# Even mixer of a two-block network: causal mask by TensorE, modulation rows by ScalarE, another order of sums, taps and output pieces

## The chip, the cores and the metric

The program runs on one core of a Trainium2 chip. Its engines are TensorE (PE in the profile, with its weight loads as PEld), VectorE (DVE), ScalarE (ACT), GpSimd (POOL) and SyncE (SP), which here issues nearly all DMAs. The metric is the device time of one execution in microseconds (us), lower is better.

## The reference, cut to what matters

The program computes two transformer-like blocks on 256 tokens of width 1024. The change lies in one stage of the first block, the even mixer, and in the modulation products that are computed beside it:

```python
mod = cond @ mod_w[layer] + mod_b[layer]            # six vectors of 1024 for each layer
h = rms_norm(x, mix_norm_g[layer]) * (1 + sc1) + sh1

def even_mixer(h, ...):
    a_val, a_gate, q, k, v = split(h @ in_w)         # 512 columns each
    u = a_val * sigmoid(a_gate)
    u = causal_dwconv(u, dw_w, dw_b)                 # 31 taps
    u = silu(layer_norm(u, ln_g, ln_b))
    q, k = rms_norm(heads(q)), rms_norm(heads(k))    # 8 heads of 64
    o = stick_breaking_attention(q, k, v)
    return concatenate([u, o]) @ out_w

# stick_breaking_attention, for one block of 128 queries
z = q @ k.T * scale
causal = kpos < qpos
log_1m = where(causal, log_sigmoid(-z), 0)
between = reverse_cumsum(log_1m) - log_1m
wts = where(causal, exp(log_sigmoid(z) + between), 0)
```

After the mixer come a gated mixture of experts (MoE), a second layer with another mixer, and the second block. They are not touched.

## The kernel before, in words

Every engine runs a list of its own, written out by hand, in order; semaphores join them. There is no scheduler. An instruction that waits holds up all that stands behind it on its engine.

Weights come from a plan (`weight_plan`): pieces of 1 MB, in the order in which TensorE uses them, through eight buffers. SyncE issues the DMA of piece i as soon as TensorE has finished with piece i - 8 (L593). A piece that is "split" is rounded by ScalarE (`act_round`, L633, two halves) and its rest computed by VectorE (`dve_half`, L650, two halves) before TensorE uses it three times over; pieces of `mod_w` are used raw.

Modulation is cut into 24 halves, numbered q. For each: TensorE multiplies the two weight pieces into four 32-row strips (`mod_half`, 8 matmuls), someone copies the 512-wide bank into a row buffer with two places (`mod_copy`, L668 on VectorE, L770 on ScalarE), TensorE sums the strips (`mod_sums`, one matmul of 512 columns for a gate, four of one column otherwise), and VectorE makes the final vector (`mod_vector`, L678 for a gate, else L682 to L688). Halves 4 to 15 run beside the even mixer. Before, VectorE copies rows 4 to 11 and ScalarE rows 12 to 15. A copy of row q waits until the sum of q - 2 is done; the products of q + 1 wait for the vector of q - 1 (`mod_half`).

In the even mixer the scores of all heads stand in six banks, z 0 to 2 for even heads and z 3 to 5 for odd ones; one of each three (2 and 5) holds the second half of the keys against the second half of the queries. ScalarE computes |z|, exp and log (L860 to L868), VectorE adds max(z, 0) to make L and multiplies the diagonal blocks by a 0/1 mask (`below`), TensorE adds the running sums onto the banks ("R", matmuls with `ntri` and `nones`), VectorE adds -1e30 above the diagonal (`negdiag`), ScalarE takes exp (L873, L874), TensorE multiplies by the values (semaphore `even_o`), ScalarE and VectorE split the result (catTh L877, catTl).

All this time VectorE works through the convolution: 31 taps, each four operations on 128x256 (L1246 with x4 per tap). The calls `conv(n)` place n taps in VectorE's list. When all are done TensorE computes mean and variance over channels, VectorE and ScalarE normalise (reciprocal L1446), and TensorE multiplies by the output weights: two pieces for rows 512 and up (from the attention), two for rows 0 to 511 (from the convolution).

Of the kernel before, what the change touches and what calls it, by code (L numbers as in the profile page):

```python
# [13 lines left out]
T = 256  # L14
# [70 lines left out]
UPTO = {"start": 2, "norm": 4, "z": 8, "R": 10, "o": 12, "x1": 14, "m0": 16, "odd": 24}  # L85


def weight_plan():
# [14 lines left out]
    def mod(l, v):  # L103
        for half in range(2):
            by_cols("mod_w", (l,), D, v * D + half * 512, 512, False)

# [106 lines left out]
    "even_dve": {"even_u": 2, "even_ss0": 1, "even_qn0": 1, "even_ss1": 1, "even_qn1": 1, "even_L": 6, "even_d": 6,  # L213
# [39 lines left out]
def mod_bank(q):  # L253

    if q < 4:
        return 4 + q
    if q == 18:
        return 1
    return (6 if q < 10 else 2 if q < 14 else 4 if q < 16 else 2) + q % 2
# [57 lines left out]
def program(nc, A, out):  # L317
    ctx = ExitStack()
    with ctx:
# [434 lines left out]
        def act_program(e):  # L754
# [66 lines left out]
            def even():  # L821
# [47 lines left out]
                for n, i in enumerate((2, 0, 1, 5, 3, 4)):  # L869
                    d = diag(L[:, i, :], i % 3)  # L870
                    e.wait_ge(*V("even_d", n + 1))
                    if i % 3 < 2:
                        e.activation(off(L[:, i, :]), off(banks[i][:, :]), ACT.Exp)  # L873
                    e.activation(d, d, ACT.Exp).then_inc(S("even_w"), 1)  # L874
# [11 lines left out]
                e.activation(sq[:, 0:T], banks[1][:, 0:T], ACT.Sqrt, scale=1.0 / 512, bias=eps).then_inc(S("even_usd"), 1)  # L886
                e.wait_ge(*V("even_un", 1))
# [5 lines left out]
                mod_copy(e, 12, copy)  # L893
# [330 lines left out]
        def dve_program(e):  # L1224
# [119 lines left out]
            def even():  # L1344
# [60 lines left out]
                for q in range(4, UPTO["z"]):  # L1405
                    mod_copy(e, q, e.tensor_copy)
                    conv(1)
                    if q > 4:
                        mod_vector(e, own, q - 1)
                for par in range(2):  # L1410
                    e.wait_ge(*V("even_ln", par + 1))
                    for i in range(3 * par, 3 * par + 3):
                        seen = own.did(stt(L[:, i, :], banks[i][:, :], 0.0, L[:, i, :], ALU.max, ALU.add))
                        own.see(seen)
                        d = diag(L[:, i, :], i % 3)
                        tt(d, d, bc(C["below"], d.shape[1]), ALU.mult).then_inc(S("even_L"), 1)
                mod_vector(e, own, 7)
                conv(2)
                for n, i in enumerate((2, 0, 1, 5, 3, 4)):
                    d = diag(L[:, i, :], i % 3)  # L1420
                    e.wait_ge(*V("even_R", 3 * (n // 3) + 3))
                    tt(d, diag(banks[i][:, :], i % 3), bc(C["negdiag"], d.shape[1]), ALU.add).then_inc(S("even_d"), 1)
                mod_copy(e, 8, e.tensor_copy)
                conv(1)
                mod_copy(e, 9, e.tensor_copy)
                conv(1)
                for i in range(2):
# [3 lines left out]
                       ).then_inc(S("even_ol"), 1)  # L1431
                mod_vector(e, own, 8)
                mod_vector(e, own, 9)
                conv(2)
                mod_copy(e, 10, e.tensor_copy)
                split_only(out(512, 0))
                mod_copy(e, 11, e.tensor_copy)
                split_only(out(512, 1))
# [527 lines left out]
        def pe_program(e):  # L1966
# [55 lines left out]
            made, summed = [0], [0]  # L2022
# [16 lines left out]
            def mod_half(q, n):  # L2039
# [3 lines left out]
                if n == 0 and q not in FIRST_MODS:  # L2043
# [9 lines left out]
            def mods_to(point):  # L2053

                for q in range(made[0], UPTO[point]):
                    mod_half(q, 0)
                    mod_half(q, 1)
                made[0] = UPTO[point]

# [29 lines left out]
            def start():  # L2089
# [9 lines left out]
                made[0] = UPTO["norm"]  # L2099
# [8 lines left out]
            def even():  # L2108
# [26 lines left out]
                for par in range(2):  # L2135
                    r = slice(64 * par, 64 * par + 64)
                    for j in range(2):
                        for m in range(2):
                            ins = mm(e, banks[3 * par + j][:, m * T:(m + 1) * T], kT[r, 2 * j + m, 0:128],
                                     qT[r, 2 * j + m, :], m == 0, m == 1)  # L2140
                        ins.then_inc(S("even_z"), 1)
                    for m in range(4):
                        ins = mm(e, banks[3 * par + 2][:, m * 128:(m + 1) * 128], kT[r, m, 128:256], qT[r, m, 128:256],
                                 m == 0, m == 3)
                    ins.then_inc(S("even_z"), 1)
# [12 lines left out]
                mods_to("R")  # L2158
# [23 lines left out]
                ins.then_inc(S("even_mean"), 1)  # L2182
                e.wait_ge(*V("even_usq", 1))
# [514 lines left out]
```

## Time and profile before

| | |
|---|---|
| median of 3 runs | 1945.02 us (1941.83 to 1945.78) |
| profiled execution | 1945.16 us, its span 1943.3 us |
| even mixer in the trace | scores from 98.9 us, last output piece ends at 194.5 us |
| TensorE busy | 1863.9 us (96% of the span) |
| VectorE busy | 1346.6 us (69%) |
| ScalarE busy | 1098.8 us (57%) |

A share of busy time is an average over the whole span. In a stage the question is which engine the others wait for: in a timeline each row gives the start, the time from start to end of that group, the engine, what it does, how many instructions, and in brackets how long the engine had been idle and what ended the idle time. TensorE's fp32 matmuls appear as two instructions each (16 matmuls are x32). Busy times of matmuls overlap and their ends are modelled, so the pace is read from one start to the next.

### The profile page before, as it was taken

What the parts mean: (1) busy time and instruction counts of PE and PEld (TensorE: products, weight loads), DVE (VectorE), ACT (ScalarE), POOL (GpSimd) and SP (SyncE); (2) the same over time, 40 slices, a digit from 0 to 9 for tenths busy, and PEclk for the clock granted to TensorE, in tenths of its full rate; (3) what the DMA queues carried; (4) which work ended last, traced back from release to release, by engine and by line L of the source; (5) the groups of instructions that cost most, each with busy time, mean ns of one, the idle gap of its engine ahead of it and who ended that gap; (6) DMA issues with size and microseconds to landing.
All of it is one profiled execution on the core that took longest, in us unless ns stands there. A gap on an engine that the chain in (4) does not pass through costs nothing.

```text
span 1943.3 us, 27022 instructions
## 1 busy us (share of the span) xinstructions
PE 1863.9 (96%) x11125; PEld 1596.8 (82%) x11125; DVE 1346.6 (69%) x1756; ACT 1098.8 (57%) x1463; POOL 51.3 (3%) x54
## 2 busy tenths in 40 slices
PE   6988899999999899999999999999999999999998
PEld 4845788888778788888799987799989998789997
DVE  3786788888777688888856565566566555656655
ACT  4443677777658577777654446654445444655443
POOL 0000011000000010000000000000000000000000
PEclk9989899999999899999999999999999999989999
DMA  9767599999967589999945565355555556425551
GB/s 362 245 241 278 207 317 335 342 335 326 335 233 278 216 324 327 340 340 325 334 136 191 195 195 169 108 174 195 195 183 186 193 191 196 157 94 181 186 192 48
DMA packets 209322, 456.98 MB, mean 235 GB/s; under 512 B 8848, under 2 KB 20776, under 8 KB 209192
## 3 DMA queue, kind: packets, MB, share of 16 engines
q1 hardware_dynamic: 206416, 451.74, 66.5%
q10 hardware_dynamic: 2776, 3.43, 0.5%
q8 instruction: 91, 1.49, 0.3%
q14 instruction: 39, 0.32, 0.1%
HBM read 454.09 MB, written 1.05 MB: 234 GB/s over the span
## 4 chain that ended last, share of the span: by engine, by line
PE 90%; DVE 4%; ACT 3%; issue 1%; DMA 1%; SPq 1%; POOL 0%; ACTq 0%; DVEq 0%; POOLq 0%
PE bank L308 88%; PE bank L1990 2%; DVE rest L650 1%; PE bank L2265 1%; DMA raw<-in_mod_w 1%; SPq L593 1%; DVE arena L1246 1%; DVE arena L1238 0%; ACT round L633 0%; ACT hTh L799 0%; ACT arena L765 0%; ACT arena L1127 0%; DVE htokl L1238 0%; DVE xres L1238 0%; DVE hTl L1238 0%
## 5 line engine op out<-in xcount | busy, mean ns | idle before, releaser
L650 DVE TENSOR_TENSOR rest<-raw,round 128x1024 fp32r<-128x1024 f32 (+1 forms) x760 | 888.5, 1218 | 256.9 <-ACT round L633 256.5
L633 ACT ACTIVATE round<-raw 128x1024 fp32r<-128x1024 f32 (+1 forms) x760 | 759.2, 1050 | 404.1 <-PE bank L308 387.9
L308 PE MATMUL bank<-hTh,round 128*128 128x256 f32 x1600 | 449.3, 281 | 11.6 <-DVE hTl L1246 3.9
L308 PE MATMUL bank<-hTl,round 128*128 128x256 f32 x1600 | 446.7, 279 | 0.0
L308 PE MATMUL bank<-hTh,rest 128*128 128x256 f32 x1600 | 446.5, 279 | 0.0
L308 PEld LDWEIGHTS bank<-hTh,round 128*128 128x128 f32 x1600 | 304.1, 190 | 16.9 <-issue 10.8
L308 PEld LDWEIGHTS bank<-hTl,round 128*128 128x128 f32 x1600 | 305.1, 191 | 1.2 <-issue 0.5
L308 PEld LDWEIGHTS bank<-hTh,rest 128*128 128x128 f32 x1600 | 303.9, 190 | 0.0
L308 PE MATMUL bank<-round,hTh 128*128 128x512 f32 x464 | 186.3, 402 | 7.2 <-DVE hTl L1238 2.9
L308 PE MATMUL bank<-round,hTl 128*128 128x512 f32 x464 | 182.6, 394 | 0.0
L308 PE MATMUL bank<-rest,hTh 128*128 128x512 f32 x464 | 181.6, 391 | 0.0
L308 PE MATMUL bank<-round,catTh 128*128 128x512 f32 x384 | 155.3, 405 | 6.6 <-DVE catTl L1238 3.5
L308 PE MATMUL bank<-round,catTl 128*128 128x512 f32 x384 | 152.5, 397 | 0.0
L308 PE MATMUL bank<-rest,catTh 128*128 128x512 f32 x384 | 151.5, 395 | 0.0
L308 PE MATMUL bank<-round,uTl 128*128 128x512 f32 x352 | 138.8, 394 | 0.0
L308 PE MATMUL bank<-rest,uTh 128*128 128x512 f32 x352 | 138.2, 392 | 0.0
L308 PE MATMUL bank<-round,uTh 128*128 128x512 f32 x352 | 137.2, 390 | 0.0
L308 PEld LDWEIGHTS bank<-round,hTh 128*128 128x128 f32 x464 | 87.3, 188 | 28.9 <-DVE hTl L1238 3.4
L308 PEld LDWEIGHTS bank<-round,hTl 128*128 128x128 f32 x464 | 87.2, 188 | 19.6
L308 PE MATMUL bank<-round,xgh 128*128 128x512 f32 x256 | 102.4, 400 | 0.0
L308 PEld LDWEIGHTS bank<-rest,hTh 128*128 128x128 f32 x464 | 87.3, 188 | 18.3 <-issue 0.5
L308 PE MATMUL bank<-round,xgl 128*128 128x512 f32 x256 | 100.9, 394 | 0.0
(221 smaller groups left out, 2169.6 us busy)
## 6 DMA issues: line engine op xcount, KB each, us to landing
raw<-in_ex_w SPq DMA_DIRECT2D x192, 1024.0 KB, 5.4
raw<-in_mod_w SPq DMA_DIRECT2D x48, 1024.0 KB, 7.5
raw<-in_ffn_w_gate SPq DMA_DIRECT2D x44, 1024.0 KB, 5.0
raw<-in_ffn_w_up SPq DMA_DIRECT2D x44, 1024.0 KB, 5.1
raw<-in_ffn_w_down SPq DMA_DIRECT2D x44, 1024.0 KB, 4.8
raw<-in_w_in SPq DMA_DIRECT2D x20, 1024.0 KB, 5.1
raw<-in_ev_in_w SPq DMA_DIRECT2D x10, 1024.0 KB, 13.0
raw<-in_od_in_w SPq DMA_DIRECT2D x8, 1024.0 KB, 5.7
```

The source lines that it names most:

```text
L308: return e.matmul(o, l, r, start=start, stop=stop, skip_group_check=True)
L593: e.dma_start(shape_of(t, k, n), a[r0:r0 + 128 * k, c0:c0 + n].rearrange("(k p) n -> p k n", p=128)).then_inc(landed, 16)
L633: e.activation(hi[:, h], raw[:, h], ACT.Copy).then_inc(S("hi"), 1)
L650: e.tensor_tensor(lo[:, h], raw[:, h], hi[:, h].bitcast(F32), ALU.subtract).then_inc(S("lo"), 1)
L1246: return e.scalar_tensor_tensor(out=o, in0=a, scalar=s, in1=b, op0=op0, op1=op1)
L1990: return e.transpose(o, i, ident)
L2265: ins = e.transpose(banks[b][:, f * CAP:(f + 1) * CAP], muf[0:CAP, f * 128:(f + 1) * 128], ident[0:CAP, 0:CAP])
```

## The change

- The diagonal mask is added to the scores by TensorE, as a matmul of the identity with `negdiag` at the end of each z bank. VectorE's six products with `below` and six sums with `negdiag` go, and ScalarE takes exp of a whole bank at once (six operations in place of ten, in the order 0, 2, 1, 3, 5, 4).
- Rows 4 to 11 are copied by ScalarE instead of VectorE.
- The halves are placed anew: 4 and 5 ahead of the running sums, 6 and 7 behind them, 8 and 9 behind the values (in banks 2 and 3, without waiting for sums), 10 and 11 behind the upper output pieces, 12 between mean and variance, 13 behind the variance. The weight plan follows this order: the two output pieces for rows 512 up come after half 9 instead of after half 11.
- Taps: before 5, 9, 1, 1, 1, 1, 2, 1, 1, 2, 7; now 5, 9, 3, 2, 4, 8.
- The upper output pieces are rounded and split earlier in ScalarE's and VectorE's lists (one ahead of the split of the attention result, one behind it), the vectors of 8 and 9 stand ahead of the last taps.

The core of the diff, TensorE's part in full:

```diff
@@ weight_plan
     mods(0)
     square("ev_in_w", (0,), 0, 5)
-    mods(1)
+    for q in (4, 5, 6, 7, 8, 9):
+        mod_of(q)
     parts("ev_out_w", (512,))
-    mod(*MODS[2][0])
+    for q in (10, 11, 12, 13):
+        mod_of(q)
     parts("ev_out_w", (0,))
-    mod(*MODS[2][1])
+    for q in (14, 15):
+        mod_of(q)
@@ act_program, even
                     e.activation(L[:, p3, :], L[:, p3, :], ACT.Ln, bias=1.0).then_inc(S("even_ln"), 1)
-                for n, i in enumerate((2, 0, 1, 5, 3, 4)):
-                    ...
+                    mod_copy(e, 4 + par, copy)
+                for i in (0, 2, 1, 3, 5, 4):
+                    e.wait_ge(*V("even_R", 3 * (i // 3) + (3 if i % 3 else 2)))
+                    e.activation(L[:, i, :], banks[i][:, :], ACT.Exp).then_inc(S("even_w"), 1)
+                act_only(e, ahead, out(512, 0))
+                mod_copy(e, 6, copy)
                 for i in range(2):
                     e.wait_ge(*V("even_o", i + 1))
                     e.activation(catT[0][:, 4 + 2 * i:6 + 2 * i, :], two(banks[i][:, :]), ACT.Copy
                                  ).then_inc(S("even_oh"), 1)
-                act_only(e, ahead, out(512, 0))
+                mod_copy(e, 7, copy)
                 act_only(e, ahead, out(512, 1))
+                mod_copy(e, 8, copy)
+                mod_copy(e, 9, copy)
                 act_only(e, ahead, out(0, 0))
+                mod_copy(e, 10, copy)
+                mod_copy(e, 11, copy)
                 act_only(e, ahead, out(0, 1))
@@ pe_program, mod_half
-                if n == 0 and q not in FIRST_MODS:
+                if n == 0 and q not in FIRST_MODS and q not in (8, 9):
@@ pe_program, even
                         for m in range(2):
-                            ins = mm(e, banks[3 * par + j][:, m * T:(m + 1) * T], kT[r, 2 * j + m, 0:128],
-                                     qT[r, 2 * j + m, :], m == 0, m == 1)
-                        ins.then_inc(S("even_z"), 1)
+                            mm(e, banks[3 * par + j][:, m * T:(m + 1) * T], kT[r, 2 * j + m, 0:128],
+                               qT[r, 2 * j + m, :], m == 0, False)
+                        mm(e, diag(banks[3 * par + j][:, :], j), ident, bc(C["negdiag"], 2), False, True
+                           ).then_inc(S("even_z"), 1)
...
                 e.wait_ge(*V("even_sig", 2))
-                mods_to("z")
-                mod_sums(UPTO["z"])
+                mod_two(4)
+                mod_two(5)
+                mod_sums(5)
                 for par in range(2):
+                    if par:
+                        mod_sums(6)
...
-                mods_to("R")
+                mod_two(6)
+                mod_two(7)
...
-                mod_sums(UPTO["R"])
-                mods_to("o")
+                mod_two(8)
+                mod_two(9)
+                mod_sums(8)
                 e.wait_ge(*V("even_ol", 2))
                 part("ev_out_w", 512, 0, True, False)
-                e.wait_ge(S("mod"), UPTO["R"])
+                mod_sums(9)
+                e.wait_ge(S("mod"), 8)
                 part("ev_out_w", 512, 1, True, False)
-                mod_sums(UPTO["o"])
+                mod_two(10)
+                mod_two(11)
                 e.wait_ge(*V("even_conv", 1))
...
                 ins.then_inc(S("even_mean"), 1)
+                mod_two(12)
...
                 ins.then_inc(S("even_var"), 1)
-                mods_to("x1")
+                mod_two(13)
                 part("ev_out_w", 0, 0, False, True, lambda c: V("even_ul", c // 2 + 1))
-                mod_sums(UPTO["x1"])
+                mod_sums(14)
```

VectorE's list, from the last taps' neighbourhood. Before, the row copy stands between the split of the upper output pieces and the last 28 tap operations; `modc` rows are modulation vectors, `mrow` the row buffer, `arena` x28 the taps, `arena<-bank 128x1024` what uses the mean:

```order
L1238 TENSOR_TENSOR catTl<-bank,catTh 128x512 [waits s_even_act] x2
...
L1246 SCALAR_TENSOR_TENSOR arena<-arena,cols 128x256 [waits s_dve] x8
L668 COPY mrow<-bank 128x512 [waits s_mod_sum,s_used]
L650 TENSOR_TENSOR rest_93<-raw_85,round_100 128x1024 [waits s_hi] x2
L668 COPY mrow<-bank 128x512 [waits s_mod_sum,s_used]
L650 TENSOR_TENSOR rest_94<-raw_86,round_101 128x1024 [waits s_hi] x2
L1246 SCALAR_TENSOR_TENSOR arena<-arena,cols 128x256 [waits s_dve] x28
L1246 SCALAR_TENSOR_TENSOR arena<-bank,arena 128x1024 [waits s_even_pe]
L682 TENSOR_TENSOR modc<-bank,cols 128x4 [waits s_mod_sum] x2
```

The same place now (lines have moved by 7 to 11):

```order
L657 TENSOR_TENSOR rest_97<-raw_89,round_100 128x1024 [waits s_hi] x2
L1257 SCALAR_TENSOR_TENSOR arena<-arena,cols 128x256 [waits s_dve] x8
L1249 TENSOR_TENSOR catTl<-bank,catTh 128x512 [waits s_even_act] x2
L657 TENSOR_TENSOR rest_98<-raw_90,round_101 128x1024 [waits s_hi] x2
...
L1257 SCALAR_TENSOR_TENSOR arena<-arena,cols 128x256 [waits s_dve] x16
L689 TENSOR_TENSOR modc<-bank,cols 128x4 [waits s_mod_sum]
...
L695 TENSOR_TENSOR modc<-modc,cols 128x4 [waits s_dve]
L689 TENSOR_TENSOR modc<-bank,cols 128x4 [waits s_mod_sum]
...
L1257 SCALAR_TENSOR_TENSOR arena<-arena,cols 128x256 [waits s_dve] x32
L1257 SCALAR_TENSOR_TENSOR arena<-bank,arena 128x1024 [waits s_even_pe]
L689 TENSOR_TENSOR modc<-bank,cols 128x4 [waits s_mod_sum] x2
```

The copies are gone, the split of the first upper piece stands ahead of the split of the attention result, and the vector of half 9 (the second row with `s_mod_sum` ahead of x32) stands ahead of the last 32 tap operations.

TensorE's list from behind the upper output pieces to the variance. Before (`cst,mrow` are sums, `arena,cst 128x256` mean and variance, `raw,cond` products of the halves):

```order
L308 MATMUL bank<-cst,mrow 128x1 [waits s_mod_row]
L308 MATMUL bank<-cst,mrow 128x1 x3
L308 MATMUL bank<-cst,mrow 128x1 [waits s_mod_row]
L308 MATMUL bank<-cst,mrow 128x1 x3
L308 MATMUL bank<-arena,cst 128x256 [waits s_even_dve]
L308 MATMUL bank<-arena,cst 128x256 x3
L308 MATMUL bank<-arena,cst 128x256 [waits s_even_act]
```

The same place now:

```order
L315 MATMUL bank<-raw_83,cond_59 32x512 [waits s_raw0,s_mod,s_start_dve]
...
L315 MATMUL bank<-cst,mrow 128x1 [waits s_mod_row,s_start_dve]
...
L315 MATMUL bank<-raw_85,cond_59 32x512 [waits s_raw2,s_mod]
...
L315 MATMUL bank<-arena,cst 128x256 [waits s_even_dve]
L315 MATMUL bank<-arena,cst 128x256 x3
L315 MATMUL bank<-cst,mrow 128x1 [waits s_mod_row,s_start_dve]
L315 MATMUL bank<-cst,mrow 128x1 x3
L315 MATMUL bank<-raw_87,cond_59 32x512 [waits s_raw4,s_mod]
...
L315 MATMUL bank<-arena,cst 128x256 [waits s_even_act]
```

The first `cst,mrow` row of the second list is the sum of half 9, which VectorE's vector ahead of the last taps waits for; it stands behind both upper output pieces and half 10. The sum of half 10 and the products of half 12 stand between mean and variance, and the sum of half 11 comes behind the variance.

## Rows read from the trace of the kernel before

**Rows 1.** The page's busy times, in us and share of the span.

```profile
PE 1863.9 (96%) x11125; PEld 1596.8 (82%) x11125; DVE 1346.6 (69%) x1756; ACT 1098.8 (57%) x1463; POOL 51.3 (3%) x54
```

**Rows 2.** Busy time by stretch: length, PE, PEld, DVE, ACT, POOL, clock, DMA share, GB/s.

```profile
97.00:152.00 55.00, 42.97 (x254) 22.15 (x252) 48.26 (x112) 23.70 (x35) 0.00 (x0) 0.84 0.70 259
152.00:207.00 55.00, 46.74 (x255) 35.31 (x256) 33.67 (x65) 20.72 (x33) 0.70 (x1) 0.91 0.75 271
300.00:400.00 100.00, 100.00 (x473) 83.01 (x472) 87.09 (x95) 73.92 (x87) 6.61 (x4) 1.00 0.93 336
```

**Rows 3.** Timeline of VectorE, 95 to 180 us.

```profile
95.51 14.34 DVE L1246 SCALAR_TENSOR_TENSOR arena<-arena,cols 128x256 f32<-128x256 f32 x36
...
117.59 0.69 DVE L668 COPY mrow<-bank 128x512 f32<-128x512 f32 x1 [2.05 <-PE bank L308]
...
124.77 0.68 DVE L1246 SCALAR_TENSOR_TENSOR arena<-bank,arena 128x512 f32<-128x512 f32 x1
...
125.83 0.68 DVE L1246 SCALAR_TENSOR_TENSOR arena<-bank,arena 128x512 f32<-128x512 f32 x1
...
131.66 0.16 DVE L682 TENSOR_TENSOR modc<-bank,cols 128x4 f32<-128x4 f32 x1
...
137.32 1.35 DVE L1238 TENSOR_TENSOR arena<-bank,cst 128x512 f32<-128x512 f32 x3 [1.08 <-PE bank L308]
...
143.57 1.44 DVE L1238 TENSOR_TENSOR catTl<-bank,catTh 128x512 fp32r<-128x512 f32 x2
...
149.82 2.35 DVE L650 TENSOR_TENSOR rest<-raw,round 128x1024 fp32r<-128x1024 f32 x2
...
154.95 11.19 DVE L1246 SCALAR_TENSOR_TENSOR arena<-arena,cols 128x256 f32<-128x256 f32 x28
168.68 1.23 DVE L1246 SCALAR_TENSOR_TENSOR arena<-bank,arena 128x1024 f32<-128x1024 f32 x1 [2.54 <-PE bank L308]
...
173.59 1.75 DVE L1446 RECIPROCAL arena<-arena 128x256 f32<-128x256 f32 x1 [1.28 <-ACT arena L886]
```

**Rows 4.** Timeline of TensorE, 95 to 181 us.

```profile
98.87 7.69 PE L308 MATMUL bank<-arena 64*128 64x256 f32 x32 [1.28 <-ACT arena L839]
106.49 6.10 PE L308 MATMUL bank<-raw,cond 128*32 128x512 f32 x32
112.52 1.12 PE L308 MATMUL bank<-mrow,cst 128*128 128x512 f32 x2
...
128.35 8.93 PE L308 MATMUL bank<-arena,cst 128*128 128x512 f32 x20 [4.04 <-DVE arena L1238]
137.21 3.64 PE L308 MATMUL bank<-raw,cond 128*32 128x512 f32 x32
140.78 2.87 PE L308 MATMUL bank<-arena 128*64 128x256 f32 x32
...
152.32 0.64 PE L308 MATMUL bank<-round,catTh 128*128 128x512 f32 x1 [3.09 <-DVE rest L650]
...
164.97 1.84 PE L308 MATMUL bank<-cst,mrow 128*128 128x1 f32 x16
166.67 1.97 PE L308 MATMUL bank<-arena,cst 128*128 128x256 f32 x8
...
180.10 0.76 PE L308 MATMUL bank<-round,catTh 128*128 128x512 f32 x1 [3.49 <-DVE catTl L1238]
```

**Rows 5.** Timeline of ScalarE, at the log and at an output piece.

```profile
110.12 2.86 ACT L868 ACTIVATE arena<-arena 128x1536 f32<-128x1536 f32 x2
...
146.55 2.00 ACT L633 ACTIVATE round<-raw 128x1024 fp32r<-128x1024 f32 x2 [0.36 <-DMA raw<-in_ev_out_w]
```

**Rows 6.** Busy time by stretch, columns as in rows 2.

```profile
106.00:109.00 3.00, 3.00 (x15) 0.85 (x18) 3.00 (x9) 2.84 (x5) 0.00 (x0) 0.50 0.00 0
127.00:130.00 3.00, 1.65 (x2) 0.84 (x3) 2.90 (x6) 0.00 (x0) 0.00 (x0) 0.50 1.06 412
```

**Rows 7.** The page's DMA issues: count, size, median us from issue to landing.

```profile
raw<-in_ex_w SPq DMA_DIRECT2D x192, 1024.0 KB, 5.4
```

More of the change, by code:

```diff
@@ L83 @@
 FIRST_MODS, LAST_MODS = (16, 17, 18), (22, 23)
-UPTO = {"start": 2, "norm": 4, "z": 8, "R": 10, "o": 12, "x1": 14, "m0": 16, "odd": 24}
+UPTO = {"norm": 4, "m0": 16, "odd": 24}
 def weight_plan():
@@ L105, in mod, with mod_of @@
             by_cols("mod_w", (l,), D, v * D + half * 512, 512, False)
+    def mod_of(q):
+        l, v, half = MOD_HALVES[q]
+        by_cols("mod_w", (l,), D, v * D + half * 512, 512, False)
     def mods(stage):
@@ L258, in mod_bank @@
         return 1
-    return (6 if q < 10 else 2 if q < 14 else 4 if q < 16 else 2) + q % 2
+    return (6 if q < 8 else 2 if q < 14 else 4 if q < 16 else 2) + q % 2
 def sum_bank(q):
@@ L886, in even @@
                 e.activation(sq[:, 0:T], banks[1][:, 0:T], ACT.Sqrt, scale=1.0 / 512, bias=eps).then_inc(S("even_usd"), 1)
+                mod_copy(e, 12, copy)
                 e.wait_ge(*V("even_un", 1))
@@ L892, in even @@
                     e.activation(catT[0][:, 2 * i:2 * i + 2, :], eu[:, 2 * i:2 * i + 2, :], ACT.Copy).then_inc(S("even_uh"), 1)
-                mod_copy(e, 12, copy)
                 mod_copy(e, 13, copy)
@@ L1404, in even @@
                 conv(9)
[L1405 to L1409, printed above, removed]
                 for par in range(2):
@@ L1412, in even @@
                     for i in range(3 * par, 3 * par + 3):
[L1413 to L1417, printed above, removed]
-                conv(2)
[L1419 to L1426, printed above, removed]
+                        stt(L[:, i, :], banks[i][:, :], 0.0, L[:, i, :], ALU.max, ALU.add).then_inc(S("even_L"), 1)
+                mod_vector(e, own, 4)
+                mod_vector(e, own, 5)
+                conv(3)
+                split_only(out(512, 0))
+                conv(2)
                 for i in range(2):
@@ L1431, in even @@
                        ).then_inc(S("even_ol"), 1)
+                split_only(out(512, 1))
+                mod_vector(e, own, 6)
+                mod_vector(e, own, 7)
+                conv(4)
                 mod_vector(e, own, 8)
                 mod_vector(e, own, 9)
[L1434 to L1438, printed above, removed]
                 conv(31)
@@ L2020, in chan_major @@
                         first()
-            made, summed = [0], [0]
+            summed = [0]
             def mod_sums(n):
@@ L2051, in mod_half, with mod_two @@
                 ins.then_inc(S("used"), 1)
[L2053 to L2058, printed above, removed]
+            def mod_two(q):
+                mod_half(q, 0)
+                mod_half(q, 1)
             def norm(j):
@@ L2098, in start @@
                         mod_sums(q)
-                made[0] = UPTO["norm"]
                 e.wait_ge(S("rows"), row_dmas)
@@ L2186, in even @@
                 ins.then_inc(S("even_var"), 1)
[L2187 removed]
+                mod_two(13)
                 part("ev_out_w", 0, 0, False, True, lambda c: V("even_ul", c // 2 + 1))
[L2189 removed]
+                mod_sums(14)
                 part("ev_out_w", 0, 1, False, True)
                 e.wait_ge(S("even_x"), 2)
[L2192 removed]
+                mod_two(14)
+                mod_two(15)
                 norm(1)
```

18 lines of the change are left out of this document (5 added, 13 removed).

## The prediction, made before the changed kernel ran

> **What bounds the kernel now.** I read the page's busy times first, then the busy time by stretch, then the timelines of VectorE, TensorE and ScalarE through the even mixer. Over the span TensorE is busy 96% [rows 1], and in the MoE stage behind the mixer it is busy 100.00 of 100 us while the DMA engines still have a little room (0.93) [rows 2]. So what the mixer gains or loses is handed on: nothing behind it absorbs it, and it starves nobody behind it. In the mixer itself TensorE is not the limit: from 97 to 152 us it is busy 42.97 of 55, VectorE 48.26 [rows 2]. TensorE waits there for VectorE three times that matter: 4.04 us ahead of the running sums, 3.09 ahead of the first output piece, 3.49 ahead of the third [rows 4]. The mean starts at 166.67, when TensorE has just ended its sums [rows 4], and the last tap ended at 154.95 + 11.19 = 166.14 [rows 3]. VectorE and TensorE thus arrive there together: a gain needs both to be earlier, a loss only one of them to be late.
>
> **The change, part by part.** I follow one path with the span's clock, before and after.
>
> *Masks on TensorE.* Six matmuls, 4 x 256 + 2 x 512 = 2048 columns. The scores are 3072 columns and take 98.87 to 106.49, 7.62 us [rows 4], mostly at a granted clock of 0.50 [rows 6], which is 1.2 GHz: 2.5 ns a column, so the masks take 5.1 us. Bounds: the running sums are 4096 columns in 8.86 us (128.35 to 137.21) [rows 4]; about 3.4 us of that stood at 0.50 [rows 6], and without it they would take 7.2, 1.75 ns a column. So 3.6 us at 2.4 GHz, and twice that, 7.2, at 1.2. I take 5.1, since the masks stand in the same stretch. Nothing hides them: |z| on ScalarE waits for each bank. Scores end at 111.6 instead of 106.5. In return go six products with `below` and six sums on VectorE.
>
> *Log and L.* The first log ended at 110.12 + 2.86/2 = 111.55 [rows 5], 5.06 after the scores. Now 116.7; VectorE has finished 36 tap operations at 109.85 [rows 3] and idles 6.8 us, a new wait. A row copy stands between the logs on ScalarE (about 0.6), so the second log ends at 118.7, and three `max` operations of 0.61 (the pair with `below` had 1.06) [rows 3] end L at 120.6. Before it was 131.66 [rows 3], behind four row copies and the waits between them (2.05 us twice). So L is 11 us earlier. This is the real gain.
>
> *Running sums.* TensorE has ended halves 4 and 5 by then, and starts at 118.6; 7.2 us plus the gate sum of half 5, 1.1 [rows 4], end at 126.9 instead of 137.2. I take the full clock, as the idle time ahead is about 2 us here and was 4.04 where the clock had fallen [rows 4, 6]; at half clock to begin with it is 1.7 us more.
>
> *Output piece and attention result.* The DMA of the first upper output piece is issued when the first half of product 6 is done, 126.9 + 0.9 = 127.8, for the buffer is that one. It lands 5.4 us later as the median piece of the MoE [rows 7], at 133.2. ScalarE rounds it (2.0 us, its first half after 1.0) [rows 5] ahead of copying row 6 and splitting the attention result; VectorE, in order, has 3 taps, then waits some 5 us for the piece, a second new wait, then 2.35 for its rest [rows 3], 2 taps of 4 x 0.40 (11.19/28) [rows 3] = 3.2, then 1.44 for catTl [rows 3]: 134.2 + 2.35 + 3.2 + 1.44 = 141.2. TensorE has had the values (2.87) and halves 8 and 9 (3.64) [rows 4] done by about 139 and waits for this. The upper pieces start at 141.3 instead of 152.32 [rows 4].
>
> *The wait on half 9.* The two pieces took 12.65 us (152.32 to 164.97) [rows 4], some 3.6 of it at half clock, so 5.4 each at full clock. TensorE: piece 5.4, sum of half 8 0.85 ((166.67 - 164.97)/2) [rows 4], piece 5.4, half 10 1.8 (3.64/2) [rows 4], sum of half 9 0.85: 155.7. VectorE has its 23rd tap done at about 150 and then stands at the vector of half 9 until 155.7, though that vector is of use to nobody but half 11. Behind that waiting instruction are the last 8 taps, 32 x 0.40 = 12.8 us, and 0.6 for the vector: taps end at 169.1, where they ended at 166.14. The work that VectorE lost (eight copies of 0.61 to 0.69, six products, six sums at 1.35 for three [rows 3], about 10.8 us) is more than paid back in three waits of 6.8, 5 and 5.5. The mean starts 169.1 - 166.67 = 2.4 us late.
>
> *From mean to reciprocal.* Before, 166.67 to 173.59, 6.92 us [rows 3, 4]; the sums of 10 and 11 were done and both halves 12 and 13 ran behind the variance. Now: mean; subtraction 1.23; vector of 10; half 12 1.8; variance 1.97; sum of 11 0.85; its vector 0.15; and only then, since VectorE's list is in order, the rest of the third output piece, 2.35 [rows 3], which before lay beside the variance; then the reciprocal. The mean comes after some 11 us of idle TensorE, so I price it at half clock, 3.45 instead of 1.97. In all 3.45 + 1.23 + 0.25 + 1.8 + 1.97 + 0.85 + 0.15 + 2.35 = 12.1 us, the reciprocal at 181.2 instead of 173.59: 7.6 late. From there to the third output piece it is 6.5 us in both (173.59 to 180.10) [rows 3, 4]. TensorE's idle time ahead of it is 7 us rather than 3.49, so a little more of the piece at half clock: 0.4.
>
> On the idle time: where TensorE had been idle 4.04 us, the running sums behind it stood at 0.50 [rows 4, 6]. The Trainium skill, page "TensorE: Matmul & The Clock Gate", section "What's actually happening", says that the slow clock is the default and that activity releases it. By that rule the 11 us ahead of the mean give the slow clock back; if the full clock were kept, the sum would be 1.9 us less. The trace agrees at the running sums.
>
> *Sum.* +2.4 (taps) +1.5 (slow mean) +0.8 (product 12 on the path and sum 11, against the waits that went) +2.9 (rest of the third piece uncovered) +0.4 = +8.0 us. Row copies on ScalarE cost nothing else: it was idle 31 of 55 us [rows 2] and each copy stands ahead of its sum with time to spare. The profiled execution took 1945.16, 1.9 over its span; with +8.0 it is 1953.2, and from the median of 1945.02 1953.0.
>
> **The rivals.**
>
> *A, VectorE's work decides (faster).* If neither the output piece nor the sum of half 9 holds VectorE, it has after L 1.2 for two gate vectors, 68 tap operations 27.1, two pieces 4.7, catTl 1.4, other vectors 1.5: taps end at 120.6 + 35.9 = 156.5, the mean 10.2 us early, at full clock; the tail still costs 12.1 - 1.5 - 6.9 = 3.7. That is 1938.5. For it: VectorE is the engine that TensorE waits for in three places. Against: the sum of half 9 would have to be there at 143.7, when TensorE by its own list is at the first output piece. The sign changes when VectorE's waits behind L come to less than about 6 us together; I count 12.6 (some 5, 5.5, and small ones). The Trainium skill, page "Perfetto Trace Analysis", section "Identifying the Most-Contended Engine", bids one shorten the busiest engine, by occupancy. That is VectorE in this stretch, so by the rule this change should be faster. The rule agrees with rows 2 and not with the order of the lists.
>
> *B, the clock stays full (no change).* The half clock at the scores may depend on how TensorE is loaded, and the masks load it more. At 1.75 ns a column scores and masks end at 107.8, 3.8 earlier than forecast, and with a fast mean and no extra slow piece the loss is 8.0 - 3.8 - 1.9 = 2.3 us: 1947.3. Against it: rows 6 show 0.50 in the middle of the scores with TensorE busy all the time.
>
> *C, the clock stays low for longer.* Idle gaps of about 2.4, 11 and 7 us. If half clock holds through the mean, sum 10, half 12, variance, and the first upper piece starts slow too, add 0.85 + 1.8 + 1.7 + 1.8: +14, 1959.2.
>
> **How the numbers follow.** Forecast 60%, B 12%, C 15%, A 10%, other 3%. The likeliest alone reaches from 1949.5 (masks at 3.6 us, landing quicker, sums as counted) to 1957 (masks at 7.2, running sums slow by 1.7). The range must take in C and part of B: 1945.5 to 1960.5. About 0.2%, 3.9 us, is what a measurement can tell from no change. Slower by more than that: the forecast, C, and little else, 75%; within it: B and the low end of the forecast, 15%; faster: A, 10%.
>
> **What would show it.** Right: L ends near 120.6; VectorE idle about 7 us ahead of its first `max` and about 5 ahead of the rest of the first upper piece; a wait of 4 to 7 us ended by TensorE at a `modc` row ahead of the last 32 tap operations; TensorE idle about 10 us ahead of the mean; the rest of the third output piece behind the variance; the reciprocal near 181; the MoE moved by the same amount. Wrong: no wait at that `modc` row, or the mean before 166.7, or a MoE stage that starts late by less than the mixer ends late.

## The result, and the profile after

The changed kernel takes 1967.0 us (median of 8 runs, 1953.26 to 1973.83) against 1945.4 of the kernel before in the same measurement: 1.0107 of it, 95% interval 1.0087 to 1.0127. Forecast were 1953.0 and the range 1945.5 to 1960.5. The sign holds and so do the places of the new waits; the loss is 21.6 us instead of 8.0, and 1967.0 lies outside the range. The profiled execution took 1971.79 us, its span is 1969.9.

The page's busy times of the changed kernel answer to [rows 1], the two stretches of the mixer to [rows 2]:

```profile
PE 1884.4 (96%) x11137; PEld 1610.3 (82%) x11137; DVE 1336.1 (68%) x1736; ACT 1101.9 (56%) x1467; POOL 52.8 (3%) x54
```

```profile
97.00:152.00 55.00, 49.01 (x235) 25.75 (x234) 34.29 (x76) 26.54 (x37) 0.00 (x0) 0.80 0.56 206
152.00:207.00 55.00, 36.37 (x174) 24.34 (x173) 29.41 (x63) 13.04 (x18) 0.00 (x0) 0.76 0.66 234
```

VectorE is busy 10.5 us less over the span, as counted (10.8), and its share of the mixer falls from 48.26 of 55 us to 34.29: the work is gone and waits stand in its place. TensorE is busy 20 us more with only twelve more matmul records (the six masks): most of that time is slower work, not more work. Its granted clock is 0.76 in the second stretch where it was 0.91.

VectorE's timeline of the changed kernel, for [rows 3]:

```profile
124.25 3.74 DVE L1257 SCALAR_TENSOR_TENSOR arena<-bank,arena 128x512 f32<-128x512 f32 x6 [12.71 <-ACT arena L875]
...
142.02 2.36 DVE L657 TENSOR_TENSOR rest<-raw,round 128x1024 fp32r<-128x1024 f32 x2 [5.79 <-ACT round L640]
...
166.30 0.16 DVE L689 TENSOR_TENSOR modc<-bank,cols 128x4 f32<-128x4 f32 x1 [7.90 <-PE bank L315]
...
166.78 12.75 DVE L1257 SCALAR_TENSOR_TENSOR arena<-arena,cols 128x256 f32<-128x256 f32 x32
183.40 1.22 DVE L1257 SCALAR_TENSOR_TENSOR arena<-bank,arena 128x1024 f32<-128x1024 f32 x1 [3.87 <-PE bank L315]
...
191.31 0.16 DVE L689 TENSOR_TENSOR modc<-bank,cols 128x4 f32<-128x4 f32 x1 [6.25 <-PE bank L315]
191.39 2.35 DVE L657 TENSOR_TENSOR rest<-raw,round 128x1024 fp32r<-128x1024 f32 x2
193.66 1.75 DVE L1443 RECIPROCAL arena<-arena 128x256 f32<-128x256 f32 x1
```

The three forecast waits stand in the forecast places: ahead of L (forecast 6.8, measured 12.71), ahead of the upper piece (about 5, 5.79), and ahead of the vector of half 9 (5.5, 7.90), with the 32 tap operations right behind it. The rest of the third piece stands right ahead of the reciprocal, as forecast.

TensorE's timeline of the changed kernel, for [rows 4], with four of the twelve groups of scores and masks (`arena` scores, `cst` masks):

```profile
108.79 2.07 PE L315 MATMUL bank<-arena 64*128 64x256 f32 x4
110.79 1.22 PE L315 MATMUL bank<-cst 128*128 128x256 f32 x2
111.94 2.07 PE L315 MATMUL bank<-arena 64*128 64x256 f32 x4
...
117.10 2.07 PE L315 MATMUL bank<-cst 128*128 128x512 f32 x2
119.10 4.05 PE L315 MATMUL bank<-raw,cond 128*32 128x512 f32 x32
...
126.19 3.71 PE L315 MATMUL bank<-arena,cst 128*128 128x512 f32 x10 [0.31 <-DVE arena L1257]
...
148.80 0.80 PE L315 MATMUL bank<-round,catTh 128*128 128x512 f32 x1 [2.79 <-DVE catTl L1249]
...
156.85 0.95 PE L315 MATMUL bank<-cst,mrow 128*128 128x1 f32 x8
...
179.59 3.78 PE L315 MATMUL bank<-arena,cst 128*128 128x256 f32 x8 [10.75 <-DVE arena L1257]
183.16 1.71 PE L315 MATMUL bank<-cst,mrow 128*128 128x1 f32 x8
185.12 3.45 PE L315 MATMUL bank<-raw,cond 128*32 128x512 f32 x16 [0.25 <-DVE modc L689]
188.50 1.99 PE L315 MATMUL bank<-arena,cst 128*128 128x256 f32 x8
```

And the clock, busy time by stretch of the changed kernel (columns as in rows 2), for [rows 6]:

```profile
103.00:106.00 3.00, 3.00 (x9) 1.72 (x8) 3.00 (x9) 0.61 (x2) 0.00 (x0) 0.50 0.01 3
...
115.00:118.00 3.00, 3.00 (x10) 2.28 (x10) 0.00 (x0) 0.60 (x1) 0.00 (x0) 0.50 0.00 0
148.00:151.00 3.00, 2.20 (x5) 1.82 (x6) 3.00 (x5) 0.00 (x0) 0.00 (x0) 0.50 1.05 409
...
184.00:187.00 3.00, 2.75 (x17) 1.35 (x20) 0.79 (x2) 2.32 (x2) 0.00 (x0) 0.50 0.00 0
223.00:229.00 6.00, 6.00 (x31) 6.00 (x29) 0.93 (x2) 2.85 (x5) 0.00 (x0) 0.50 1.05 406
```

Stage by stage, from the starts of the rows (us; each line runs from the event ahead of it, and the sums are of unrounded values):

| up to | before | forecast | changed | off |
|---|---|---|---|---|
| last score or mask, from the first score | 7.6 | 12.7 | 18.5 | +5.8 |
| first running sum | 21.9 | 7.0 | 7.1 | +0.1 |
| first upper output piece | 24.0 | 22.7 | 22.6 | -0.1 |
| mean | 14.3 | 27.8 | 30.8 | +3.0 |
| reciprocal | 6.9 | 12.1 | 14.1 | +2.0 |
| third output piece | 6.5 | 6.5 | 6.5 | 0 |
| end of the fourth | 14.4 | 14.8 | 15.4 | +0.6 |
| first expert matmul of the MoE | 27.9 | 27.9 | 30.2 | +2.3 |
| sum | 123.6 | 131.6 | 145.2 | +13.6 |

The sum differs by 21.6 us between the two traces. That this equals the difference of the medians is in part luck: the profiled run of the changed kernel is 4.8 us above its median, and the two spans differ by 26.6. Of the other 5.0 us, 1.7 lie ahead of the first score and 3.3 behind the first expert matmul, where nothing changed.

This holds for all traces of this case. Span less the stretch of the table, which is code that no kernel here changes but for the order of the weight plan and a small copy, takes between 1813.9 us (e8) and 1829.9 us (e11). So a trace tells what a stage took in that execution, and only the timed runs tell what the kernel takes.

### The profile page after: what moved, and what is told of

Its sections match the earlier page's. It is cut to its first block, busy times and chain, and to the rows that moved or that the text cites. A ratio compares the mean times of both kernels' runs of the same rounds, so it can differ in the third digit from the quotient of the medians.

```text
span 1969.9 us, 27029 instructions
## 1 busy us (share of the span) xinstructions
PE 1884.4 (96%) x11137; PEld 1610.3 (82%) x11137; DVE 1336.1 (68%) x1736; ACT 1101.9 (56%) x1467; POOL 52.8 (3%) x54
## 4 chain that ended last, share of the span: by engine, by line
PE 89%; ACT 4%; DVE 4%; issue 1%; DMA 1%; POOL 0%; SPq 0%; ACTq 0%; DVEq 0%; POOLq 0%
PE bank L315 86%; PE bank L1987 2%; DVE arena L1257 1%; DVE rest L657 1%; ACT round L640 1%; DMA raw<-in_mod_w 1%; PE bank L2269 1%; DVE arena L1249 0%; DMA raw<-in_ev_out_w 0%; ACT arena L772 0%; ACT hTh L806 0%; ACT arena L1034 0%; ACT arena L1138 0%; DVE htokl L1249 0%; DVE xres L1249 0%
## 6 DMA issues: line engine op xcount, KB each, us to landing
raw<-in_ev_in_w SPq DMA_DIRECT2D x10, 1024.0 KB, 11.7
```

## The experiments

Each result begins with the ratio to the kernel before on the same chip, with its 95% interval. Single runs of one kernel spread by 1%. The runs were made on three chips: e1 to e4 and e11 on one, e0 and e5 to e7 on another, e8 to e10 on a third. So e0 and e5 to e7 can be compared directly; elsewhere a difference to the changed kernel is one of two ratios. Where the times can't tell two kernels apart, the stages of the traces are given, one trace for each kernel, in the terms of the table.

**e0, the changed kernel again**, no edit.

> The changed kernel as it is, so that it stands on the same chip as the experiments. Theory: scores and masks again take 18 to 19 us with the clock at half nearly throughout, since that came with every kernel that has a mask behind each bank of scores (the changed one, e1, e4); 0.8 to 1.3% slower than before. Rival (the long half clock of the first trace was chance): scores and masks near 13 to 15 us in this trace, and 0.4 to 0.7% slower.

1.0122 (1.0073 to 1.0172), as expected; scores and masks took 18.3 us. One stretch of its scores, columns as in rows 2:

```profile
103.00:116.00 13.00, 13.00 (x32) 7.89 (x32) 7.17 (x19) 5.04 (x6) 0.00 (x0) 0.50 0.00 0
```

TensorE is busy 13.00 of 13 us and has half clock throughout. All six traces of kernels with a plain mask behind each bank (the changed kernel, e0, e1, e4, e6, e7) show 18.3 to 18.6 us. The other stages repeat as well: 30.4 us from the first upper piece to the mean, 13.9 to the reciprocal, 30.3 to the MoE. The first trace was not chance.

**e1, masks alone in the kernel before.**

```diff
-                        ins.then_inc(S("even_z"), 1)
+                        mm(e, diag(banks[3 * par + j][:, :], j), ident, bc(C["negdiag"], 2), False, True
+                           ).then_inc(S("even_z"), 1)
...
-                        tt(d, d, bc(C["below"], d.shape[1]), ALU.mult).then_inc(S("even_L"), 1)
...
-                    tt(d, diag(banks[i][:, :], i % 3), bc(C["negdiag"], d.shape[1]), ALU.add).then_inc(S("even_d"), 1)
```

> The kernel before with the masks on TensorE alone (six mask matmuls, exp of whole banks; products with below and sums with negdiag gone from VectorE). Theory: masks stand at half clock and each change between 64-row scores and 128-row masks costs TensorE about 0.3 us, so scores and masks take about 18.5 us as after the change, not 7.6, and all behind moves by 10.9 less the 5.9 us of VectorE work that goes: 4 to 8 us slower than before. Rival (the forecast's price of 5.1 us was right and the loss lies in the order of the lists): scores and masks take about 12.7 us and the kernel is within 2 us of before.

1.0006 (0.9988 to 1.0024), so 4 to 8 us slower did not come; the medians are 1.5 us apart. In the trace scores and masks took 18.6 us, as the theory said, and from the first score to the MoE it is 131.5 us against 123.6, 8 more: 11.0 for scores and masks, less 0.8 in the stages behind and 2.3 in the approach to the MoE (the table's last stage). Stage and time disagree. The two traces come from different measurements: the kernel before had a median of 1945.4 us where its trace was taken and 1952.17 on the chip of e1, and there is no trace of it there. So the price of the masks is shown in the stage, and what they cost this kernel in total stays open.

**e2, the changed kernel with the masks on VectorE.**

```diff
-                        mm(e, diag(banks[3 * par + j][:, :], j), ident, bc(C["negdiag"], 2), False, True
...
+                        tt(d, d, bc(C["below"], d.shape[1]), ALU.mult).then_inc(S("even_L"), 1)
...
+                    tt(d, diag(banks[i][:, :], i % 3), bc(C["negdiag"], d.shape[1]), ALU.add).then_inc(S("even_d"), 1)
```

> The changed kernel with the masks back on VectorE (products with below, sums with negdiag, exp in pieces); order, row copies and weight plan stay changed. Theory: scores end 11 us earlier, L is 2.7 us longer, the waits behind it stay: 8 us faster than the changed kernel, so 12 to 14 us slower than before. Rival (the order is nearly all of the loss): at most 5 us faster than the changed kernel.

1.0060 (1.0036 to 1.0083), 9 us under the changed kernel's 1.0107 and 11.7 over before, close to the theory. From the first upper piece to the mean it is still 29.9 us, to the reciprocal 13.9. So without the masks more than half of the loss stays: the order, the row copies and the weight plan together. The scores took 5.1 us, all at full clock:

```profile
101.05 5.16 PE L315 MATMUL bank<-arena 64*128 64x256 f32 x32 [1.28 <-ACT arena L846]
```

They are the same instructions as in the kernel before, behind the same 1.28 us of idle time, and there they took 7.62 us, with the clock at half from 2.4 us behind the first one. So whether the clock falls within the scores is not set by this code alone, and 2.5 us of what this trace gains in the scores are not the masks' doing.

**e3, masks grouped**: in each half of the heads three banks of scores, then three masks.

```diff
-                        mm(e, diag(banks[3 * par + j][:, :], j), ident, bc(C["negdiag"], 2), False, True
-                           ).then_inc(S("even_z"), 1)
...
+                    for j in range(3):
+                        mm(e, diag(banks[3 * par + j][:, :], j), ident, bc(C["negdiag"], 4 if j == 2 else 2), False, True
+                           ).then_inc(S("even_z"), 1)
```

> The changed kernel with the three masks of each half of the heads behind its three banks of scores, so 4 changes between 64-row and 128-row matmuls in place of 12. Theory of a price per change of 0.3 us: scores and masks take 16.1 instead of 18.5 us and the kernel is about 2 us faster than the changed one. Rival (only clock and columns count): 18.5 us, no gain.

1.0032 (0.9999 to 1.0066), seven runs from 1947.61 to 1968.4; by the medians it is 11 us slower than before, by the ratio 6, so the size of the gain is loose. Scores and masks took 12.7 us: neither the 16.1 of the theory nor the 18.5 of the rival. That is 5.8 less than interleaved, and fewer changes account for 2.4 of it. The end of them:

```profile
106.00:110.00 4.00, 4.00 (x8) 2.13 (x8) 4.00 (x11) 1.37 (x3) 0.00 (x0) 0.50 0.00 0
110.00:114.70 4.70, 4.70 (x25) 3.45 (x25) 2.92 (x8) 4.27 (x5) 0.00 (x0) 0.98 0.00 0
```

Here the clock came back within the stage, 7 us after it fell; that is the rest of the gain, and no experiment shows what brought it back.

**e4, the vector of half 9 ahead of the last tap.**

```diff
                 mod_vector(e, own, 8)
+                conv(7)
                 mod_vector(e, own, 9)
                 conv(31)
```

> The changed kernel with the vector of half 9 placed ahead of the last tap instead of ahead of the last eight. Theory (the wait of 7.9 us there is paid by the taps): the wait goes, the taps end 7.9 us earlier, half 11 then runs in the gap ahead of the mean: 7 us faster than the changed kernel. Rival (TensorE is late itself and the wait only hides it): no more than 2 us.

1.0035 (1.0014 to 1.0055), 14 us under the changed kernel's 1.0107, where 7 were expected. By its trace the stretch is 12 us shorter than in e0. From the first upper piece to the mean it took 24.2 us instead of 30.4: the wait, 6.2. Mean to reciprocal, of which nothing was expected, fell too, from 13.9 to 10.4, and the approach to the MoE by 2.2. The rival (TensorE is late itself) falls. TensorE in e4:

```profile
171.09 3.48 PE L315 MATMUL bank<-raw,cond 128*32 128x512 f32 x16 [4.19 <-DVE modc L695]
174.50 1.99 PE L315 MATMUL bank<-arena,cst 128*128 128x256 f32 x8
```

Half 11 now stands right ahead of the mean and takes the slow start (3.48 us), and the mean is fast (1.99, it was 3.78). The wait cost twice: its own length, and the clock that it took from what followed.

**e5, rounded masks**, in the old places: the identity and the mask as fp32r.

```diff
+                e.tensor_copy(negr[:, :], C["negdiag"])
-                        mm(e, diag(banks[3 * par + j][:, :], j), ident, bc(C["negdiag"], 2), False, True
+                        mm(e, diag(banks[3 * par + j][:, :], j), identr[:, :], bc(negr[:, :], 2), False, True
```

> The changed kernel with the six masks as rounded fp32 matmuls (identity and mask copied once to that type), which run at about a quarter of the time per column of the plain ones. Theory (the masks' price is their columns at half clock and the path passes it on): 6.8 us of mask columns become 1.7, scores and masks 12 to 13.5 us, kernel 5 to 8 us faster than the changed one. Rival (the change between 64-row and 128-row matmuls holds the clock low and costs most of it): at least 16 us, at most 2 us faster.

1.0099 (1.0070 to 1.0127) against 1.0122 of the changed kernel on the same chip, 4.4 us by the medians, just under the range expected; the intervals overlap, so the times can't tell this from no gain. By the traces the mean stands 70.8 us behind the first score instead of 79.7. Scores and masks took 8.5 us, 9.8 less and well under the 12 to 13.5 expected, since they stood at full clock throughout. All twelve changes are still there, so they do not hold the clock low by themselves, and the rival as it was put (at least 16 us) falls. That the rounded masks kept the clock up is not shown: in e2 the scores had full clock too, and in e8 to e11, with rounded masks in groups, it fell.

**e6, the tail as before.**

```diff
+                mod_sums(12)
                 e.wait_ge(*V("even_conv", 1))
...
-                mod_two(12)
                 e.wait_ge(*V("even_usq", 1))
...
+                mod_two(12)
                 mod_two(13)
```

> The changed kernel with the sums of halves 10 and 11 ahead of the mean and half 12 behind the variance, as before; vectors 10 and 11 and the rest of the third output piece then lie beside the variance. Theory: from mean to reciprocal 14.1 us become 8 to 9 (one slow mean), 5 us faster than the changed kernel. Rival (those parts were hidden anyway): no difference.

1.0103 (1.0067 to 1.0139), 3.2 us faster by the medians on one chip, which is within the noise. In the trace mean to reciprocal took 10.1 us instead of 13.9. That is short of the 8 to 9 expected, since both mean (3.78) and variance (3.37) stood at half clock.

**e7, TensorE kept busy ahead of the mean.**

```diff
+                for _ in range(20):
+                    mm(e, banks[1][:, 0:T], ones, bc(C["iota"], 2), True, True)
                 e.wait_ge(*V("even_conv", 1))
```

> The changed kernel with 20 matmuls of constants (256 columns each, result unused) in TensorE's idle gap ahead of the mean. Theory (the gap gives the full clock back): mean 2.0 instead of 3.6 us, sum 10 and half 12 2.8 instead of 5.2, mean to reciprocal 10 instead of 14 us, kernel 4 us faster than the changed one. Rival (the clock falls there for another reason, or the added work holds the mean up): no gain, or a loss of up to 2 us.

1.0128 (1.0097 to 1.0159) against 1.0122, with the median 1.9 us lower: the 4 us expected don't show in the times. They show in the stage. TensorE in e7:

```profile
178.51 1.99 PE L315 MATMUL bank<-arena,cst 128*128 128x256 f32 x8 [1.92 <-DVE arena L1257]
180.34 0.95 PE L315 MATMUL bank<-cst,mrow 128*128 128x1 f32 x8
181.88 1.92 PE L315 MATMUL bank<-raw,cond 128*32 128x512 f32 x16 [0.60 <-DVE modc L689]
```

The mean took 1.99 us for 3.78, the sum 0.95 for 1.71, half 12 1.92 for 3.45, and mean to reciprocal 10.4 for 13.9. With the gap filled the clock stays up, so it is the idle gap that took it.

**e9, rounded and grouped masks alone in the kernel before** (e1 with the edits of e3 and e5).

> The kernel before with the masks alone, rounded and grouped. Theory (TensorE masks pay where they are short): scores and masks 8 to 11 us instead of 7.6, VectorE 5.9 us of work less on the path of L and of the weights: 2 to 5 us faster than before. Rival: no difference to e1, which had them long and interleaved.

1.0010 (0.9990 to 1.0030): no gain, and no different from e1, as the rival said. Scores and masks took 10.9 us, and from there to the running sums 20.2 instead of 21.9. VectorE's list in e9 shows where most of its 5.9 us went: into a wait ahead of the row copy of half 8, where the kernel before waited 0.53 us:

```profile
143.43 0.69 DVE L669 COPY mrow<-bank 128x512 f32<-128x512 f32 x1 [6.72 <-PE bank L308]
```

**e10, three repairs of the changed kernel**: masks as in e9, the tail of e6, five taps between the vectors of 8 and 9.

> The changed kernel with three repairs: masks rounded and grouped; five taps more ahead of vector 9 (three left behind it); the tail of e6. Theory: 8 to 10 us from the masks, 5 to 7 from the taps, 4 to 5 from the tail, so 17 to 22 us faster than the changed kernel and within 4 us of before. Rival (the parts overlap and share one gain): no more than 10 us faster than the changed one.

1.0027 (1.0004 to 1.0050), 16 to 18 us faster than the changed kernel's 1.0107 and 1.0122, so the rival falls; from the first score to the MoE it is 128.4 us, 17 less than in the changed kernel. The sum came out near the forecast, but not from its parts. The masks gave 7.7 us and the tail 5.2, the taps 2 instead of 5 to 7, and the approach to the MoE 3 that nobody had forecast. VectorE ended its last tap at about 165.0 (160.14 + 4.83), and the mean started only at 170.55:

```profile
167.12 3.57 PE L315 MATMUL bank<-cst,mrow 128*128 128x1 f32 x16 [4.92 <-ACT mrow L778]
170.55 3.76 PE L315 MATMUL bank<-arena,cst 128*128 128x256 f32 x8
```

The tail of e6 puts the sums of 10 and 11 ahead of the mean, and these wait for ScalarE's row copies. In ScalarE's list the copies stand behind the rounding of the third output piece, which waited for its DMA until 164.58. In e6 the same wait (4.73) lay in the gap ahead of the late taps; here the taps are early and it shows. One repair uncovered a wait that another had brought.

**e8, another order.** Its core, beside the masks of e9:

```diff
-                conv(9)
+                conv(11)
-                conv(3)
+                conv(6)
                 split_only(out(512, 0))
-                conv(2)
...
-                mod_vector(e, own, 9)
                 conv(31)
+                mod_vector(e, own, 9)
...
@@ ScalarE
+                mod_copy(e, 10, copy)
                 act_only(e, ahead, out(0, 0))
-                mod_copy(e, 10, copy)
-                mod_copy(e, 11, copy)
                 act_only(e, ahead, out(0, 1))
...
@@ TensorE, (mean) and (variance) stand for their matmuls
-                mod_two(11)
+                mod_sums(11)
                 (mean)
-                mod_two(12)
+                mod_two(11)
                 (variance)
+                mod_two(12)
                 mod_two(13)
```

> A version meant to beat both: masks rounded and grouped behind each half's scores; taps 5, 11, 6, 4, 5 so that VectorE's waits hold taps; vector 9 behind the last tap, half 11 between mean and variance, halves 12 and 13 behind the variance, the rest of the third output piece ahead of vector 11. Theory (each of the changed kernel's waits was paid by taps standing behind them): scores and masks 8.5 to 11 us, mean 52 to 58 us behind the first score (before 67.8, changed 79 to 80), mean to reciprocal 7 to 8; 9 to 13 us faster than before. Rival (the clock takes it back, since TensorE idles more): within 3 us of before.

0.9960 (0.9942 to 0.9978), 8 us faster than before and just under the 9 to 13 expected. The mean stands 56.4 us behind the first score (67.8 before, 79.0 changed), inside the forecast, but mean to reciprocal is 14.0, not 7 to 8. ScalarE in e8:

```profile
159.44 2.00 ACT L641 ACTIVATE round<-raw 128x1024 fp32r<-128x1024 f32 x2 [5.21 <-DMA raw<-in_ev_out_w]
162.00 2.00 ACT L641 ACTIVATE round<-raw 128x1024 fp32r<-128x1024 f32 x2 [0.55 <-DMA raw<-in_ev_out_w]
163.91 1.04 ACT L895 ACTIVATE arena<-arena 128x1024 f32<-128x1024 f32 x1
```

The square (163.91) needs only VectorE's subtraction, which ended at about 158.6. It stands behind two roundings that wait for a DMA.

**e11, the square ahead of the roundings.**

```diff
-                act_only(e, ahead, out(0, 0))
-                act_only(e, ahead, out(0, 1))
                 e.wait_ge(*V("even_uc", 1))
                 e.activation(usq, eu, ACT.Square).then_inc(S("even_usq"), 1)
+                act_only(e, ahead, out(0, 0))
                 mod_copy(e, 11, copy)
...
+                act_only(e, ahead, out(0, 1))
                 mod_copy(e, 12, copy)
```

> e8 with ScalarE's square (for the variance) ahead of rounding the third output piece, and the fourth piece rounded behind the root. In e8 the square stood behind both roundings, whose DMAs are issued only when half 10 is done: mean to variance 9.7 us. Theory (a wait in ScalarE's list like those in VectorE's): mean to variance 2.5 us, mean to reciprocal 8 instead of 14 us, third output piece 6 us earlier, 4 to 7 us faster than e8, 0.6 to 0.8% faster than before. Rival (half 11 or the piece itself, not the square, sets it): no more than 1 us.

0.9935 (0.9914 to 0.9957), 12.6 us faster than before and 5 faster than e8 by the ratios, as expected. From the first score to the MoE it is 114.3 us, the shortest of all (e8 119.2), though the profiled run was the slowest of its nine: its 1829.9 us outside this stretch were the longest. Mean to variance took 4.4 us for 9.7 (2.5 expected), mean to reciprocal 8.5 for 14.0:

```profile
158.93 1.97 PE L315 MATMUL bank<-arena,cst 128*128 128x256 f32 x8
160.83 1.92 PE L315 MATMUL bank<-raw,cond 128*32 128x512 f32 x16
163.30 1.99 PE L315 MATMUL bank<-arena,cst 128*128 128x256 f32 x8 [0.55 <-ACT arena L893]
```

## Why the prediction was wrong in size and right in kind

*Masks, 5.1 us: the step that failed most.* They cost 10.9 in this stage. I priced them at the mean pace of the scores, 2.5 ns a column, which mixed full and half clock. The full-clock part at the beginning is used up by the first 2.4 us of scores, and added columns lengthen the half-clock part. The row of 106 to 109 that I read for this covers only the last half microsecond of the scores; these rows of the kernel before cover more of them (first the stretch, then the starts of two records in a row, each from a narrow window of the timeline):

```profile
103.00:106.00 3.00, 3.00 (x12) 2.63 (x11) 3.00 (x9) 2.99 (x4) 0.00 (x0) 0.50 0.00 0
...
102.51 1.06 PE L308 MATMUL bank<-arena 64*128 64x256 f32 x2
102.94 1.06 PE L308 MATMUL bank<-arena 64*128 64x256 f32 x2
```

Two records of one 256-column matmul start 0.43 us apart, and each matmul has two of them, so a matmul takes 0.85 us, 3.3 ns a column: 6.8 us for 2048 columns. My upper bound of 7.2 held that. The rest is mostly a price that I had nowhere: each change between 64-row scores and 128-row masks. The four score records from 108.79 take 2.00 us where four times 0.43 is 1.71, so 0.29 a change, twelve of them 3.5 us. The Trainium skill, page "TensorEngine Tiling (Array Packing)", section "Key Properties", says that a change of tiling mode drains the engine; the 0.29 us agree with that. The remaining 0.6 us I can't place. What the masks' stage cost in total time is less sure than the stage itself (e1, e5).

*Log, L, running sums, output piece: right.* 7.1 and 22.6 us against 7.0 and 22.7. The new wait on the output piece's DMA was 5.79 (forecast about 5).

*The wait on half 9: right in place, 3.0 us short.* The first upper piece took 8.05 us (148.80 to 156.85), not 5.4, which is 2.7 of the 3.0: the clock was 0.50 from its start, after 2.79 us idle. I had let rival C hold that (1.8) and left it out of the sum. e4 shows that the wait and the taps behind it are real.

*Mean to reciprocal: right in its parts, 2.0 short.* I had priced the mean at half clock and let half 12 run at full (1.8); it took 3.45, which is 1.6 of the 2.0. e6 and e7 show both halves of the stage, the order and the clock, at about 3.5 to 4 us each.

*"What the mixer loses is handed on": right, but not that it is handed on exactly.* Norm and router behind the mixer took 30.2 us for 27.9. The rows show half clock at 223 to 229. The same stage reads 25.7 to 30.3 in kernels that do not differ there, and the mean granted clock goes with it: 0.87 over e1's 25.7 us, 0.76 over the 27.9 before, 0.66 over these 30.2. So what differs there is the clock and not the code.

Of the signs that I had named, the waits, their places and the idle time ahead of the mean (10.75) came; three numbers did not: L ended at 128.0 and not near 120.6, the wait at the vector of half 9 was 7.90 and not 4 to 7, and the reciprocal started at 193.66 and not near 181.

Of the rivals, A (faster) fell with the result itself, and the wait that it needed gone is there (7.90). B fell in both traces of the changed kernel. C, the longer half clock, is nearest to what came: 14 us were its price, 21.6 the truth. It had the first upper piece and half 12 right in kind, and a slow variance that did not come (1.99). It lacked 5.8 us of the masks and 2.3 of the approach to the MoE. That a time beyond even C's came in the forecast's direction is not to the credit of the forecast: its mechanism named the places of the loss and priced most of them at too high a clock. C had 15%; it should have been part of the forecast.

What stays open is what sets the clock in the scores. From its fall within the scores TensorE, busy without a gap, was granted half clock for 17 us in all six traces with interleaved plain masks, for 10 us in the kernel before, e8, e9 and e10, for 14 us in e11, whose masks are those of e8, and for 7 us in e3 (read in stretches of 1 us, over the scores and the products behind them). In e2 and e5 it did not fall there at all. The changes of row group alone don't do it (e5), and the code of the scores alone doesn't decide it (e2 against before).

## What to carry to other kernels

In lists that are written in order, look for what stands behind a new wait, not for how much work goes: 10.5 us of VectorE's work were removed and 21.6 us lost, about half of it because a vector that nobody needed yet held the last eight taps (e4). Price added TensorE work at the clock of the stretch in which it lands, and ask of every new gap what the work behind it costs at half clock: here the mean took 3.78 us for 1.99. When an engine is freed, move work of its own into the waits: e8 and e11, which do this and reorder the tail as well, are 0.40% and 0.65% faster than before, while e10, which only repairs, is 0.27% slower. And try repairs together: each may have been hiding another's wait (e10).

## What the runs showed of the hardware that I had not expected

- A change between 64-row and 128-row fp32 matmuls cost TensorE 0.29 us at half clock (2.00 for 1.71), and 0.21 at full clock: in e5 four score records took 1.06 us (103.36 to 104.42), where e2's pace of 5.09 us for 3072 columns gives 0.85.
- TensorE had half clock while it was busy 13.00 of 13 us (e0).
- The same score matmuls took 7.62 us in the kernel before and 5.09 in e2, by the clock alone.
- Rounded masks took scores and masks from 18.3 to 8.5 us at the same count of matmuls (e5). Of these 9.8 us at most 5.1 are columns at half clock: a rounded 512-column matmul starts 0.43 us behind the last at half clock (before, 152.32 to 152.75), a plain one takes 1.71, so 2048 columns take 1.7 us for 6.8. The rest is the clock.
